# First norm by scaled tokens, a buffer for every early modulation chunk, a later first split, and pooling projections every fifth step

## The reference

```
mod = silu(c) @ w_ada + b_ada;  sh1, sc1, g1, sh2, sc2, g2 = split(mod)
h = rmsnorm(x, norm1_g) * (1 + sc1) + sh1
proj = h @ w_in                    # q (8 heads), k, v (2 heads), u_pool (4 groups of 128)
att = blocked_gqa(rope(norm(q)), rope(norm(k)), v)
pool = einsum(mean_over_window(u_pool, 2/4/8/16) - u_pool, w_pool) * pool_scale
x = x + g1 * (concat[att, pool] @ w_out)
h2 = rmsnorm(x, norm2_g) * (1 + sc2) + sh2;  x = x + g2 * conv_gated_ffn(h2)
```

## Time and profile before

| what | us |
|---|---|
| median of 3 runs | 1408.26 (1407.53 to 1409.25) |
| the profiled execution, its own time | 1407.91 |
| its span, first to last instruction | 1406.1 |
| PE busy in the span | 1357.9 (97%) |
| DVE, ACT, POOL busy | 771.4, 636.0, 707.0 |
| mean granted TensorE clock | 0.986 of 2.4 GHz |

### The profile page before, as it was taken

How to read it: one execution, slowest core, us unless ns; L and a number is a source line. 1 busy time by engine, 2 the same in 40 slices (tenths; PEclk the granted TensorE clock), 3 DMA queues, 4 the chain that set the end, 5 groups by cost and what they waited for, 6 DMA issues and landing times.

```text
span 1406.1 us, 17599 instructions
## 1 busy us (share of the span) xinstructions
PE 1357.9 (97%) x7007; PEld 1116.6 (79%) x7007; DVE 771.4 (55%) x1249; ACT 636.0 (45%) x1174; POOL 707.0 (50%) x382
## 2 busy tenths in 40 slices
PE   6898889999999999999999999999999999999998
PEld 6676569888888888897777777778888888888886
DVE  5578866676777664656776854325276421312224
ACT  4446545443441332635776755555554422413321
POOL 1248653565565554654333554448707654645560
PEclk8799999999999999999999999999999999999999
DMA  8323552455555564321112121124302232222321
GB/s 328 149 68 105 181 194 91 160 200 191 196 191 200 179 209 143 116 87 61 61 63 88 60 80 55 47 90 150 120 1 66 95 109 90 90 90 94 116 91 60
DMA packets 32050, 167.54 MB, mean 119 GB/s; under 512 B 3552, under 2 KB 4192, under 8 KB 18912
## 3 DMA queue, kind: packets, MB, share of 16 engines
q1 hardware_dynamic: 31968, 166.42, 34.2%
HBM read 164.31 MB, written 2.10 MB: 118 GB/s over the span
## 4 chain that ended last, share of the span: by engine, by line
PE 85%; DVE 6%; ACT 3%; POOL 2%; DMA 2%; issue 1%; SPq 0%; DVEq 0%; ACTq 0%
PE B L552 82%; PE B L972 1%; DMA ZF<-in_w_ada_rows 1%; ACT WH L1193 1%; DVE SC L1787 1%; DVE ZF L1864 1%; DVE ZF L1873 1%; DMA SC<-in_w_ada 1%; POOL WL L2302 1%; PE B L796 1%; DVE SC L1956 1%; DVE SC L1951 1%; POOL G L2340 1%; DVE ST L1973 0%; DMA RAW<-in_slabs 0%
## 5 line engine op out<-in xcount | busy, mean ns | idle before, releaser
L2302 POOL TENSOR_TENSOR WL<-RAW,WH 128x512 fp32r<-128x512 f32 (+1 forms) x203 | 474.5, 2353 | 469.4 <-ACT WH L1193 423.7
L552 PE MATMUL B<-HH,WH 128*128 128x512 f32 (+2 forms) x1040 | 403.9, 391 | 3.8 <-ACT HH L1275 2.1
L552 PE MATMUL B<-HH,WL 128*128 128x512 f32 (+2 forms) x1040 | 396.8, 384 | 0.0
L552 PE MATMUL B<-HL,WH 128*128 128x512 f32 (+2 forms) x1040 | 385.3, 382 | 0.0
L1193 ACT ACTIVATE WH<-RAW 128x512 fp32r<-128x512 f32 (+1 forms) x203 | 193.0, 981 | 195.3 <-PE B L552 178.2
L552 PEld LDWEIGHTS B<-HH,WH 128*128 128x128 f32 x1040 | 196.4, 189 | 44.2 <-issue 4.9
L552 PEld LDWEIGHTS B<-HH,WL 128*128 128x128 f32 x1040 | 196.3, 189 | 39.0
L552 PEld LDWEIGHTS B<-HL,WH 128*128 128x128 f32 x1040 | 191.4, 188 | 34.4
L552 PE MATMUL B<-ZR,WH 128*128 128x512 f32 (+1 forms) x624 | 165.0, 353 | 1.2 <-POOL WL L2302 0.7
L2314 POOL TENSOR_TENSOR ZR<-SC,ZR 128x512 fp32r<-128x512 f32 (+1 forms) x72 | 97.0, 1350 | 114.9 <-ACT ZR L1687 50.8
L1873 DVE CUSTOM_DVE_ANT_0 ZF<-ZF,VT 128x1024 f32<-128x1024 f32 x80 | 137.0, 1737 | 16.5 <-DMA ZF<-in_w_ada_rows 16.5
(11 more groups left out here) (254 smaller groups left out, 1753.9 us busy)
## 6 DMA issues: line engine op xcount, KB each, us to landing
RAW<-in_slabs SPq DMA_DIRECT2D x102, 1024.0 KB, 4.9
ZF<-in_w_ada_rows SPq DMA_DIRECT2D x80, 512.0 KB, 4.1
G<-in_w_ada SPq DMA_DIRECT2D x8, 512.0 KB, 10.2
RAW<-in_slabs SPq DMA_DIRECT2D x4, 768.0 KB, 4.4
RAW<-in_x SPq DMA_DIRECT2D x4, 512.0 KB, 7.4
SC<-in_w_ada SPq DMA_DIRECT2D x4, 512.0 KB, 9.7
ZF<-in_w_ada SPq DMA_DIRECT2D x4, 512.0 KB, 10.0
out<-SC SPq DMA_DIRECT2D x8, 256.0 KB, 2.1
```

The lines of the kernel that those rows point to most:

```text
L552: return e.matmul(out, l, r, start=start, stop=stop)
L2302: e.tensor_tensor(lo[:, at], k.RAW[:, i % 2, at], hi[:, at].bitcast(F32), ALU.subtract).then_inc(*w.hit((i, q)))
```

## The change

In the start, ACT now scales x by y while tokens are still on partitions (XS, L1268 of the new kernel), PE turns the scaled x (`scaled_x`, 32 more transposes, L707) and ACT copies it to the slots (L1277); the widening of y, its turn, RB and DVE's eight `unit` multiplications are gone. ACT's part of slab 0 is made in quarters behind the gain, and POOL's part waits for chunk 15 on DVE. SHARED is 2 instead of 3. Chunks 10 to 15 have buffers of their own in what later is HH and HL. `c_rows` stands behind the second `ada_sum`. The first slab multiplies all of HH by WH ahead of HH by WL. In the attention loop the tables are others, ACT no longer makes a second copy of a projected pooling group, and POOL scales the window sum itself (one instruction more for each group).

```diff
-SHARED = 3
+SHARED = 2
 def place(n):
-    if n < 10:
+    if n < EARLY:
         return n, None
-    return (n - 6, n - 6) if n < EARLY else (4 + n % 2, n - 6 if n < 18 else n - 2)
+    return 4 + n % 2, n - 12 if n < 18 else n - 2
-ADA1 = [*range(9, 20, 2), *range(20, 38)]
-T1 = {"q3": 0, "p0": 4, "p1": 9, "p2": 13, "p3": 18}
-POOL_OUT = {22: 0, 23: 1, 24: 2, 26: 3}
-MIX = {28: 0, 29: 1, 32: 2, 34: 3}
+ADA1 = [*range(9, 22, 2), *range(22, 39)]
+T1 = {"q3": 0, "p0": 5, "p1": 10, "p2": 15, "p3": 20}
+POOL_OUT = {24: 0, 26: 1, 28: 2, 30: 3}
...
     def first_slab(name, keys, st):
-        wh, wl = slab(name)
+        pe.wait_ge(k.sig("act_w")[k.ix[name], 3])
+        wh = k.split_of(k.ix[name])[0].rearrange("p (k n) -> p k n", k=8)
...
                 mm(b[:, :], wh[:, j, 128 * i:128 * i + 128], HH[:, j, :], j == 0, False)
+        for i, b in enumerate(bs):
+            for j in range(8):
+                _, wl = slab(name, j)
                 mm(b[:, :], wl[:, j, 128 * i:128 * i + 128], HH[:, j, :], False, False)
...
+    def scaled_x():
+        for j in range(8):
+            b = B.take(pe, "main", ("xs", j))
+            for q in range(4):
+                pe.wait_ge(sq[0, "scaled", q])
+                t = e.transpose(b[:, 128 * q:128 * q + 128], k.XS[:, q, 128 * j:128 * j + 128], k.IDN)
+            t.then_inc(*x_full.hit(("xs", j)))
...
+    for n in range(SHARED):
+        ada_chunk(n)
+    B.deal(main=(1, 2, 3, 4, 5, 6, 7))
+    scaled_x()
+    B.deal(main=(1, 2), one=(3,))
+    ada_sum(1)
+    for n in range(8, 8 + SHARED):
+        ada_chunk(n, "one")
+    ada_sum(0)
+    B.deal(main=(4, 5, 6, 7))
+    c_rows()
...
-        if s in MIX:
-            mix(MIX[s], 0, 4, ("main", "main", "s", "s")[MIX[s]])
+        if 32 <= s < 36:
+            mix(s - 32, 0, 4, ("main", "main", "s", "s")[s - 32])
...
+    pool.wait_ge(k.sig("dve_ada")[0, 7])
+    quarters()
```

More of the change, by code:

```diff
@@ L385, in __init__ @@
         self.XT = sb("XT", [128, 8, T])
+        hbase = nc.sbuf_base
         self.HH = sb("HH", [128, 8, T], F32R)
@@ L417, in __init__ @@
         self.early += [self.G[:, 1024 * i:1024 * i + 1024] for i in range(4)]
+        late = nc.alloc_sbuf_tensor_at("LATE", [128, 6144], F32, offset=hbase + 4 * 2048)
+        self.early += [late[:, 1024 * i:1024 * i + 1024] for i in (2, 3, 4, 5, 0, 1)]
+        self.XS = plain("XS", 11264, 4096)[:, :].rearrange("p (q n) -> p q n", q=4)
         self.COL = [self.M8[:, i, 0:4] for i in range(3)] + [self.M8[:, 0, 4:8]]
@@ L433, in __init__ @@
         self.WPOOL = [G[:, 1632 + 128 * i:1760 + 128 * i] for i in range(4)]
-        self.MEAN = [G[:, 2560 + 512 * i:3072 + 512 * i] for i in range(3)] + [self.slot(0)]
+        self.MEAN = [G[:, 2560 + 512 * i:3072 + 512 * i] for i in range(3)] + [self.PB[:, 16:528]]
         self.HID = [ZR[:, 8192 * i:8192 * i + 8192] for i in range(2)]
@@ L1252, in act_program @@
     e.activation(y, y, ACT.Exp, scale=-0.5).then_inc(*root_.hit(("exp", 0)))
-    def xt(j):
+    act.wait_ge(v_root["y", 0])
+    for q in range(4):
+        e.activation(k.XS[:, q, :], k.xtok[:, q, :], ACT.Copy, scale=y[:, q:q + 1]).then_inc(*sq.hit((0, "scaled", q)))
+    for j in (1, 3, 5, 7):
         act.wait_ge(x_full[j])
@@ L1257, in xt @@
         B.free(("x", j), xs["xt", j])
[L1259 to L1267, removed]
+    for j in range(8):
+        act.wait_ge(x_full["xs", j])
+        act.wait_ge(k.sig("pe_ada")[1, SHARED - 1])
+        act.wait_ge(v_ada[1, 3])
+        e.activation(k.slot(j), B["xs", j][:, :], ACT.Copy).then_inc(*xs.hit(("unit", j)))
+        B.free(("xs", j), xs["unit", j])
     for j in range(8):
         act.wait_ge(v_ada["gain", 0])
-        act.wait_ge(v_h["unit", j])
+        act.wait_ge(xs["unit", j])
         e.activation(k.slot(j), k.slot(j), ACT.Copy, scale=k.GS[:, 0, j:j + 1]).then_inc(*sq.hit(("gain", 0, j)))
+    quarters()
     for j in range(8):
@@ L1367, in act_program @@
                 act.wait_ge(proj_full[x])
[L1368 to L1371, removed]
+                e.activation(k.PA[:, 16:528], B[x][:, :], ACT.Copy).then_inc(*mix.hit(("pa", g)))
+                B.free(x, mix["pa", g])
         u = at1(s, "wide")
@@ L1914, in dve_program @@
     e.scalar_tensor_tensor(out=y, in0=tmp, scalar=1.5, in1=y, op0=ALU.add, op1=ALU.mult).then_inc(*root_.hit(("y", 0)))
-    xt(0)
+    xt(0), xt(2), xt(4), xt(6)
     dve.wait_ge(k.sig("in_vec")[0])
-    ada_chunk(SHARED)
-    xt(2)
-    ada_chunk(SHARED + 1)
-    xt(4), xt(6)
-    for n in range(SHARED + 2, 8):
+    for n in range(SHARED, 8):
         ada_chunk(n)
-    for j in range(4):
-        unit(j)
     ada_mod(1)
     gains(0, 0, 64, 1)
-    for j in range(4, 8):
-        unit(j)
     for n in range(8 + SHARED, 16):
@@ L2342, in mean_ops @@
             yield
+        pool.wait_ge(mix["win", g, w])
+        e.tensor_scalar(other[:, 16:528], src[:, 16:528], 1.0 / w, None, ALU.mult).then_inc(*mix.hit(("part", g)))
+        yield
         for c0, e0 in ((0, 0), (504, 8)):
-            pool.wait_ge(mix["win", g, w])
-            e.tensor_tensor(src[:, 16 + c0:24 + c0], src[:, 16 + c0:24 + c0], k.EDGE[:, 16 * g + e0:16 * g + e0 + 8],
+            pool.wait_ge(mix["part", g])
+            e.tensor_tensor(other[:, 16 + c0:24 + c0], src[:, 16 + c0:24 + c0], k.EDGE[:, 16 * g + e0:16 * g + e0 + 8],
                             ALU.mult).then_inc(*mix.hit(("edge", g, c0)))
@@ L2348, in mean_ops @@
         pool.wait_ge(mix["edge", g, 504])
-        pool.wait_ge(a_mix["px", g])
-        e.tensor_tensor(m, src[:, 16:528], m, ALU.subtract).then_inc(*mix.hit(("mean", g)))
-    weights()
+        e.tensor_tensor(m, other[:, 16:528], PA[:, 16:528], ALU.subtract).then_inc(*mix.hit(("mean", g)))
+    pool.wait_ge(k.sig("dve_ada")[0, 7])
+    quarters()
     weights()
@@ L2511, in sp_program @@
         load(f"in_x{q}", 0, k.xtok[:, q, :], a["x"][0, 128 * q:128 * q + 128, :])
-    for n in range(10):
+    for n in range(12):
         ada(n)
     weights()
-    for n in range(10, EARLY):
+    for n in range(12, EARLY):
         ada(n)
```

8 lines of the change are left out of this document (1 added, 7 removed).

## The result

The changed kernel takes 1399.76 us (median of 6 runs, 1396.93 to 1401.69), beside 1408.73 for the kernel before in the same session (6 runs, 1407.53 to 1409.92): the ratio is 0.9935 with a 95% interval of 0.9922 to 0.9948. Its profiled execution took 1400.29 us, with a span of 1398.5.

A forecast was written before the change was run, and what follows sets the result against it. DVE, slowed by POOL, bounds the start; in the loop PE up to step 22, then DVE. Start 4.4 plus loop 3.2 (2.0 + 3.2 - 2.0) makes 7.6 us, from 1407.91 to 1400.3; median 1400.7, range 1396 to 1406.5.

The forecast's parts named there:

- the tail: Loop from the maximum at step 30 on: four mix halves delay PE, residual 3.5 us later, cost 2.0 us (0 to 5).
- T: In the start, the time chunk 15 ends on DVE: 41.72 us before, predicted 36.0, bound by landings.
- I take the fast one: the clock had held through 5.4 us of chunk products before: Start, 32 XS transposes on PE: 4.0 us at the fast clock, not 7.1, so T is 36.0, not 38.9.
- DVE itself is the bound until T: Start of the kernel before: DVE sets when chunk 15 ends; its units cost 9.3 us, 4.3 of them contention.
- Contention by POOL: Start: POOL's big subtraction slows DVE's units by 4.3 us; afterwards the bias beside POOL costs 0.6 us (0 to 1.2).
- After T: First slab after chunk 15 on DVE: ends at T + 18.7, before T + 17.4, giving back 1.3; start gains 4.4.
- Up to step 22: Attention loop: moving p3 takes 12 products, 2.7 us of PE, out of earlier steps; step 22 comes 2.0 us earlier.
- t + 27, and with POOL's 2 us t + 29: PE reaching the last column after step 30's maximum (t): 5.5 us more products, 1.6 less waiting, POOL 2 us late.
- A: Rival: low clock in the XS transposes, DVE behind them; start gains 1.5, whole 4.7, 1403.5 us; chance 0.14.
- B: Rival: loop gives nothing or costs 1 to 2 us, POOL late; whole gain 2.9, 1405.4 us; chance 0.14.
- D: Rival: PE on the lower clock through the four mixes, some 38 products deciding; 13.6 us lost, 1414.3 us; chance 0.05.
- C: Rival: both stages give all, start 5.0 and loop 7 us; 1396.3 us; chance 0.12.

The follow-up runs named there:

- start_only: The changed kernel with the attention loop of the kernel before (tables, means and mixes as before): 1405.69 us, ratio 0.998.
- before_late_split: The kernel before with one edit, POOL's part of slab 0 waiting for chunk 15 on DVE: 1409.8 us, ratio 1.0004.
- before_buffers: The kernel before with own buffers for chunks 10 to 15, and chunks 10 and 11 issued ahead of slab 0: 1408.49 us, ratio 1.0003.
- early_split: The changed kernel with slab 0 split early: ACT's quarters ahead of the gain, no wait on POOL for chunk 15: 1401.29 us, ratio 0.9951.
- before_buffers_late_split: The kernel before with own buffers for chunks 10 to 15 and POOL's part of slab 0 waiting for chunk 15: 1405.66 us, ratio 0.9986.
- loop_only: The kernel before with the new attention loop and the old start: 1402.06 us, ratio 0.9955.
- c_rows_early: The changed kernel with c_rows put back behind the first ada_sum: 1400.79 us, ratio 0.9951.
- both_banks: The changed kernel with the first slab's HH by WH products taken over both banks in turn, not bank by bank: 1397.67 us, ratio 0.9925.
- interleaved: The changed kernel with three of the eight turned tiles of XS between PE's two chunks: 1398.44 us, ratio 0.9932.
- split_32: The changed kernel with the last two quarters of the slab split in the loop at steps 32 and 33, not 30 and 31: 1398.28 us, ratio 0.993.

## Why the prediction came out right, point by point

Predicted 1400.7, measured 1399.76; from the two profiled executions 7.6 us of gain predicted, 1407.91 - 1400.29 = 7.6 seen. By the medians of one session it is 9.0. The total is right, but partly by luck: the start gave 1.6 us less than predicted and the tail cost 1.4 more, while the loop up to step 30 gave 2.9 more. Two such misses also put the maxima of step 22 at 140.63 us, where 140.8 was predicted.

- **T: 36.0 predicted, 37.8 in the profiled run.** The step "I take the fast one: the clock had held through 5.4 us of chunk products before" failed in that run, and of the seven traces with this order of the start it held in two. The sum behind it was sound on both sides: with the clock up, 36.03, bound by the landing (start_only); with it down, DVE alone, 37.8, a little under the stated 38.9, since the clock rose again from 25 us on and DVE was back at its chunks at 30.1, not 31.7.
- **"DVE itself is the bound until T" was incomplete.** A landing at the same time as DVE's end was hidden behind it (before_late_split). The terms happened to be right because the change removed both, which is luck and no insight of the prediction.
- **Contention by POOL.** Right in kind and size: 4.1 us again when POOL's subtraction met a chunk (before_buffers), 3.8 in quarters (early_split). The bias beside POOL took 0.59 us more, predicted 0.6; it was 1.4 more in before_buffers_late_split, where POOL's subtraction is one instruction.
- **After T.** The slab ended at T + 18.6, predicted T + 18.7; the give-back was 18.57 - 17.42 = 1.15, predicted 1.3. The start gained 59.14 - 56.38 = 2.8 instead of 4.4.
- **Up to step 22: 2.0 predicted, 3.85 seen**, and 5.4 to 5.5 in the four traces where step 6 to 8 was undisturbed. The term was mis-sized. Between the maxima of steps 0 and 22 loop_only has 4.1 us less of PE's work (57.45 against 61.51) where I counted 2.7 for the 12 products, and PE idles 1.5 us less where I had taken off 0.7 for a larger bubble. The rest is the step "up to step 22 PE is the fuller engine", which fails for the kernel before at step 22 itself: there DVE was the later one. PE's scores of step 22 and the chunk that DVE had ahead of their maxima, before, and the scores in after:

```profile
145.12 0.97 PE L552 MATMUL B<-ZR 64*128 64x512 f32 x6
146.03 1.27 DVE L1873 CUSTOM_DVE_ANT_0 ZF<-ZF,VT 128x1024 f32<-128x1024 f32 x1
139.54 0.96 PE L554 MATMUL B<-ZR 64*128 64x512 f32 x6
```

  Before, the scores were done at 146.09 and the maxima began at 147.23, 1.1 us later; in after it is 0.1 us (140.50 and 140.63), in loop_only nothing. The new ADA1 has one chunk less ahead of step 22. So 2.7 (products), 1.5 (idle) and 1.1 (DVE) make up 5.3 of the 5.5 us in the undisturbed trace of loop_only. This also accounts for most of the work that I had not counted: PE turned a unit (eight transposes) in that 1.1 us ahead of the maxima before, and behind them now.
- **Steps 22 to 30: 25.8 predicted, 24.7 seen** (24.7 to 25.1 in all traces with the new loop and the new means). The pairs of steps took 5.9 to 6.7 us; DVE paces as said, and no wait for the mean was left.
- **The tail: 2.0 predicted, 3.4 seen.** The step "t + 27, and with POOL's 2 us t + 29" had POOL's delay nearly right (2.6), but not the lower clock behind the pause: 1.6 more. Where the clock held (c_rows_early, early_split) its t + 29 came. PE's last column started at 196.0, t + 30.6, and the first residual at t + 31.5, 6.2 later than before and not 3.5; norm 2 took up 2.8 of it. In three other traces with the pause and the lower clock (loop_only, both_banks, interleaved) the tail cost more, 4.7 to 5.4; in both_banks two squarings on DVE took 1.8 and 1.6 us there instead of 0.7, and why is not shown. Without the pause (split_32) the tail costs 1.8.
- **The rivals.** A's mechanism, slow transposes and DVE behind them, did come in the profiled run, and cost 1.8 us of T. Its price was hidden by the loop, which gave 4.7 instead of 3.2. B is refuted by loop_only. D did not come: the clock was low for a few us at a time (the mean from step 22 to 30 was 0.87, and before it was 0.88 as well), for 8 products in the mixes, far from 38. C did not come: the loop gave 8.1 us up to step 30, but its tail took back 3.4, and the start gave 2.8 and not 5.0. One slip of adding is of no weight: half of B and the last case make 0.12 for "same", with 0.05 for slower, not 0.11 and 0.06.

## What to carry to other kernels

Two bounds that end at the same time hide each other: an experiment that takes one away and finds nothing has not shown that it is free, and a trace shows no wait for the second. A short pause of PE may cost more than its own length: 2.6 us of waiting were followed by 1.6 of slow products in four of six traces, and by none in two. So a wait near a dense stretch has a range, not one price. Work that must be done anyway (c_rows, the second bank's products) is best put where PE follows another engine's pieces one by one. And a term read from one trace (which engine ends last at a given step) should be checked at that very step: on the average of the stage PE was the fuller engine, at step 22 DVE came later.
